# Statistics and score placement in the memory-attention stage of a decoder layer: q statistics ahead of the mix statistics, scores ahead of the up product, denominators behind it

## The chip, the cores and the metric

The program runs on all 8 cores of one Trainium2 chip. Each core computes one of the eight batch elements, all cores run the same instructions on data of their own, and the weights are shared. The metric is device time in microseconds (us) of the slowest core, the median of several executions; lower is better.

## The reference

One decoder layer over 4096 positions of width 1024: a mixer of gated linear attention and dilated window attention, then cross-attention into 256 memory tokens, then a gated MLP. The change lies in the second of the three, and in its overlap with the end of the first and the start of the third:

```python
def memory_cross_attention(h, mem, ...):
    xn = rms_norm(h, norm_x)
    mn = rms_norm(mem, norm_mem)
    q = rms_norm((xn @ w_xq).reshape(b, s, X_HEADS, X_HEAD_DIM), x_q_norm)
    k, v = jnp.split(mn @ w_xkv, 2, axis=-1)
    k = rms_norm(k.reshape(b, m, X_HEADS, X_HEAD_DIM), x_k_norm)
    p = jax.nn.softmax(jnp.einsum('bshd,bmhd->bhsm', q, k) * (X_HEAD_DIM ** -0.5), axis=-1)
    o = jnp.einsum('bhsm,bmhd->bshd', p, v).reshape(b, s, D_MODEL)
    return h + o @ w_xo
```

Before it stands `h + merged @ w_mix_out` (the mix), behind it `up = rms_norm(h) @ w_ffn_up`, a causal convolution of width 3 on the gate half, `gelu(conv) * u`, and the down product.

## The kernel before

The 4096 positions are cut into 32 tiles of 128 (`NT = 32`) and 8 blocks of 512. Every engine has one instruction list in program order; an instruction waits on semaphores for the writers of what it reads and for the readers of what it overwrites, and everything behind it on that engine waits too. So the order of the Python calls is the order on each engine, and nothing is scheduled later. All matmuls are recorded by one helper line (L249), ScalarE activations by L275, VectorE tensor-tensor operations by L282, scalar-tensor-tensor by L308, plain DMAs by L241, DMA transposes by L245.

The memory stage is a software pipeline, the loop `for k in range(5, NT + 11)` (L1817). In step k it works on several tiles and heads at once:

- `mix(i)` (L1412), only for k < 9, tiles 28 to 31: 16 matmuls of 512 columns, two VectorE adds into the tile `xt` (xtT in the trace), its store as h1, then the mix statistics: a ScalarE Square over 1024 columns with an accumulated sum (junkT), `rstd_pool` (two short GpSimd operations), and the VectorE scaling to `xs` (xsT). `x2trans` and `x2store` transpose xs by DMA through one buffer x2s and store it, `x2load` (L1534) reads it back (x2i) for the q product two steps on.
- `q_proj(k)` (L1562): 16 matmuls into two of the three PSUM banks of `PQ`. `q_stats(k)` (L1574): four Squares of 256 columns, Ln, Exp on ScalarE (jh, hnx). `q_norm(k)`: four VectorE operations that read the two banks (qn). `q_trans(k)`: a DMA transpose to qT.
- `score` (L1688) for head index k-5, a block and one of its four heads: 4 matmuls and two ScalarE Exps into a `ptsx` buffer (three of them). `denom` (L1700): 2 matmuls of a matrix of ones with ptsx, then Ln and Exp on ScalarE (lgx, rdx). `outp` (L1711): VectorE multiplies ptsx by the reciprocal denominator (pn).
- `x_out(k-10)` (L1718), the output product: 16 matmuls, two VectorE adds into the tile h1x, a store.
- From k = 32 on there is no q product. In its place stands `up(0, fc)` (L1774), 16 matmuls of the first MLP block: one ScalarE copy of the gate half (abt), which shares a buffer with a short VectorE copy of the history columns (hist) and so comes behind it, then VectorE's convolution (cv). `glu` (L1797) of the column group before does the Gelu on ScalarE (gl) and a VectorE product (yT), which frees the bank of the other half.

I call k = 32 to 36 the tail: in these five steps scores 27 to 31 are made beside `up` 0 to 4. Before the change a tail step issues on TensorE: `denom` of the last step's score, `x_out`, `up`, `score`. The banks of `score`, `denom` and `x_out` come from one rotation `P` of five; those of `up` from `PQ`. At k = 37 `P` becomes a rotation of all eight and `up` joins it; counted through, `up(5)` then gets the bank that the second half of `x_out(27)` has just filled, and `x_out(28)` gets the bank of the other half of `up(4)`. In steps 37 to 41 the four last output products run with `up` 5 to 13; after that the rest of the MLP.

Of the kernel before, what the change touches and what calls it, by code (L numbers as in the profile page):

```python
# [407 lines left out]
NT = S // 128  # L408
# [31 lines left out]
def build():  # L440
# [47 lines left out]
    def rows(i):  # L488
        return slice(i * 128, (i + 1) * 128)
# [42 lines left out]
    def rstd_pool(ss, src, dst, n, dim):  # L532
        fw.ts("pool", ss[:, dst:dst + n], ss[:, src:src + n], 1.0 / dim, ALU.mult, EPS, ALU.add)
        fw.tt("pool", ss[:, dst:dst + n], ss[:, dst:dst + n], mh[:, 0:n], ALU.pow)
# [632 lines left out]
    for c in range(NT):  # L1167
        s_, c4 = c // 4, c % 4
        nx = 1 <= s_ < NS - 1
        i = c + 8  # L1170
# [56 lines left out]
    TA = [dict() for _ in range(NT)]  # L1227
# [180 lines left out]
    def xload(i):  # L1408
        TA[i]["xt"] = xtr.next()
        fw.dma(TA[i]["xt"][:, :], x[rows(i), :])  # L1410

    def mix(i):  # L1412
        s_, t_ = i // 4, i % 4
        h1t = TA[i]["xt"]
        for half in range(2):
            cs_ = slice(half * 512, (half + 1) * 512)
            pm = P.next()
            for kc in range(8):
                fw.mm(pm[:, :], mT[s_ % 2][:, kc, t_ * 128:(t_ + 1) * 128], wmo[:, kc, cs_], start=(kc == 0), stop=(kc == 7))
            fw.tt("dve", h1t[:, cs_], pm[:, :], h1t[:, cs_], ALU.add)  # L1420
        fw.dma(V(h1_d[i], h1_d[i].t[rows(i), :]), h1t[:, :])
        ss = ogc["nss"].next()
        fw.act(ogc["junk"][:, :], h1t[:, :], AF.Square, accum=ss[:, 0:1])
        rstd_pool(ss, 0, 2, 1, 1024)
        xs = ogc["xs"].next()
        fw.ts("dve", xs[:, :], h1t[:, :], ss[:, 2:3], ALU.mult)
        TA[i]["xs"] = xs

    def x2trans(i):
        fw.dmat(x2s[:, :, :], TA[i]["xs"][:, :])  # L1430

    def x2store(i):
        fw.dma(V(xn2_d[i], xn2_d[i].t[i]), x2s[:, :, :].rearrange("p c t -> p (c t)"))
# [100 lines left out]
    def x2load(i):  # L1534
        TC[i]["x2"] = ogc["x2i"].next()
        fw.dma(TC[i]["x2"][:, :, :].rearrange("p c t -> p (c t)"), V(xn2_d[i], xn2_d[i].t[i]))
# [25 lines left out]
    def q_proj(i):  # L1562
        c = TC[i]
        xnv = c["x2"]
        pq = []
        for half in range(2):
            cs_ = slice(half * 512, (half + 1) * 512)
            p_ = PQ.next()
            for kc in range(8):
                fw.mm(p_[:, :], xnv[:, kc, :], KV["wxq"][kc // 2][:, kc % 2, cs_], start=(kc == 0), stop=(kc == 7))  # L1570
            pq.append(p_)
        c["qs"] = [pq[h // 2][:, (h % 2) * 256:(h % 2 + 1) * 256] for h in range(4)]

    def q_stats(i):  # L1574
        ss = QA["hnr"].next()
        for h in range(4):
            fw.act(V(QA["jhs"][h], QA["jh"].t[:, h, :]), TC[i]["qs"][h], AF.Square, accum=ss[:, h:h + 1])
        fw.act(ss[:, 4:8], ss[:, 0:4], AF.Ln, scale=1.0 / 256, bias=eps_c)
        TC[i]["ss"] = ss
        return fw.act(ss[:, 8:12], ss[:, 4:8], AF.Exp, scale=-0.5)  # L1580

    def q_norm(i):
        c = TC[i]
        qn = QA["qn2r"].next()
        for h in range(4):
            fw.stt("dve", qn[:, h * 256:(h + 1) * 256], c["qs"][h], c["ss"][:, 8 + h:9 + h], KV["gq"][:, :],
                   ALU.mult, ALU.mult)
        c["qn"] = qn

    def q_trans(i):  # L1590
        fw.dmat(QA["qTs"][i // 4 % 2][i % 4][:, :, :], TC[i]["qn"][:, :])
# [24 lines left out]
    for s_ in range(NS):  # L1616
        for m in range(8):
# [18 lines left out]
            if L % 2 == 1 and 8 <= (L + 9) // 2 < NT:  # L1636
                i = (L + 9) // 2
# [3 lines left out]
            if s_ > 0:  # L1641
                i = (s_ - 1) * 4 + m // 2
# [37 lines left out]
    def t1b_late():  # L1680
        XL["pn"].append([ar.at("pn1_%d" % h, (128, 2, 512), BF16, (120 + 2 * h) * K_) for h in range(4)])
        XL["xsr"] = ar_ring("xsX", 2, (128, 1024), BF16, 128 * K_)
        XL["junkX"] = ar.at("junkX", (128, 1024), BF16, 134 * K_)
# [4 lines left out]
    def score(s_, h):  # L1688
        pts = ptsr.next()
        for mb in range(2):  # L1690
            p_ = PB.next()
            for dc in range(2):
                ap = QA["qT"][s_ % 2].t[:, :, h * 2 + dc, :]
                v_ = [V(b, ap) for b in QA["qTs"][s_ % 2]]
                fw.mm(p_[:, :], kmT[:, h * 2 + dc, mb * 128:(mb + 1) * 128], v_[0], start=(dc == 0), stop=(dc == 1),
                      xr=v_[1:])
            fw.act(pts[:, mb, :], p_[:, :], AF.Exp, scale=1.0 / 16)
        SC[s_][h] = pts

    def denom(s_, h):  # L1700
        pts = SC[s_][h]
        pD = PB.next()
        for mb in range(2):
            fw.mm(pD[:, :], ones_b, pts[:, mb, :], start=(mb == 0), stop=(mb == 1))
        lg = XL["lgr"].next()
        fw.act(lg[:, :], pD[:, :], AF.Ln)
        rd = XL["rdr"].next()
        fw.act(rd[:, :], lg[:, :], AF.Exp, scale=-1.0)
        SC[s_]["rd"] = rd

    def outp(s_, h):  # L1711
        fw.tt("dve", XL["pn"][s_ % 2][h][:, :, :], SC[s_][h][:, :, :], SC[s_]["rd"][:, :].raw(0, [[0, 2], [1, 512]]), ALU.mult)
# [5 lines left out]
    def x_out(i):  # L1718
        s_, t_ = i // 4, i % 4
        c = TC[i]  # L1720
        h_ = c["h"]
        pn = XL["pn"][s_ % 2]
        for half in range(2):
            cs_ = slice(half * 512, (half + 1) * 512)
            px = PB.next()
            for kc in range(8):
                fw.mm(px[:, :], pn[kc // 2][:, kc % 2, t_ * 128:(t_ + 1) * 128], KV["MX"][kc // 2][:, kc % 2, cs_],
                      start=(kc == 0), stop=(kc == 7))
            fw.tt("dve", h_[:, cs_], px[:, :], h_[:, cs_], ALU.add)
        fw.dma(V(h2_d[i], h2_d[i].t[rows(i), :]), h_[:, :])  # L1730

    def x_stats(i):
        c = TC[i]
        h_ = c["h"]
        jk, ss = XL["junkX"], XL["nsr"].next()
        fw.act(jk[:, :], h_[:, :], AF.Square, accum=ss[:, 0:1])
        fw.act(ss[:, 1:2], ss[:, 0:1], AF.Ln, scale=1.0 / 1024, bias=eps_c)
        fw.act(ss[:, 2:3], ss[:, 1:2], AF.Exp, scale=-0.5)
        c["xss"] = ss
# [7 lines left out]
    def x3_trans(i):  # L1747
        fw.dmat(F_["x3s"][i % 4][:, :, :], TC[i]["xs"][:, :])
# [48 lines left out]
    def glu(p):  # L1797
        fc, c1, pu = p
        gl = F_["gl"].next()
        fw.act(gl[:, :], c1[:, :], AF.Gelu)  # L1800
        fw.tt("dve", ysub[fc][:, :], gl[:, :], pu[:, :], ALU.mult)
# [15 lines left out]
    for k in range(5, NT + 11):  # L1817
        pace = None
        if k < 9:
            if k < 8:  # L1820
                xload(NT - 3 + k - 5)
            mix(NT - 4 + k - 5)
        if k < 10:
            x2trans(NT - 5 + k - 5)
        if k == 9:
            t1b_late()
        if k < NT:
            q_proj(k)
            pace = q_stats(k)
        if 0 <= k - 6 < NT:  # L1830
            denom((k - 6) // 4, (k - 6) % 4)
        if 0 <= k - 5 < NT and k < NT:
            score((k - 5) // 4, (k - 5) % 4)
        if 6 < k + 2 < NT:
            x2load(k + 2)
        if k < NT:
            q_norm(k)
            q_trans(k)
        if k < 10:
            x2store(NT - 5 + k - 5)  # L1840
        if 0 <= k - 6 < NT:
            outp((k - 6) // 4, (k - 6) % 4)
        if 0 <= k - 10 < NT:
            x_out(k - 10)
        if k >= NT:
            if k == NT:
                ffn_alloc()
            if k == NT + 5:
                P.items = BK[3:8] + BK[0:3]
                PF["r"] = P  # L1850
            for _ in range(1 if k < NT + 6 else 2):
                if len(UPD) < 14:
                    cur = up(0, len(UPD))
                    if UPD:
                        glu(UPD[-1])
                    UPD.append(cur)
            if k - 5 < NT:
                score((k - 5) // 4, (k - 5) % 4)
        if 0 <= k - 10 < 4:
            x_stats(k - 10)  # L1860
            x_scale(k - 10)
            x3_trans(k - 10)
        if pace is not None:
            fw.wait_for("pool", [pace])
        if 0 <= k - 8 < NT:
            loadh(k - 8)
        if 9 <= k < NT + 1 and k % 2 == 1:
            up_load((k - 9) // 4, (k - 9) // 2 % 2)
        for fc in UP_LATE.get(k - NT, ()):
            up_load(fc)  # L1870
        if k == NT + 5:
            wdn_load(0)
        if k == NT + 6:
            wdn_load(1)
        if k == NT + 7:
            wdn_load(2)
# [26 lines left out]
    for s_ in range(NS):  # L1903
# [12 lines left out]
        for t_ in range(4):  # L1916
            i = s_ * 4 + t_
# [69 lines left out]
```

How the kernel before makes its waits and increments, by code:

```python
            def run(eng, acts, s):  # L368
                for a in acts:
                    if a[0] == "w":
                        eng.wait_ge(a[1], a[2])
                    else:
                        ins = a[1]
                        bi = ins.fn(eng)
                        if ins.dma:
                            bi.then_inc(dsem[ins.dsem], 16)
                        elif ins.signal:
                            bi.then_inc(esem[s], 1)
```

## Time and profile before

| what | value |
|---|---|
| median of 3 runs | 2854.3 us (2852.8 to 3007.62) |
| the profiled execution's own time | 2852.89 us |
| its span, core 0, the slowest | 2851.3 us (the cores: 2839.6 to 2851.3) |
| TensorE busy | 2752.4 us (97%), 15208 matmuls |
| VectorE, ScalarE, GpSimd busy | 1734.0 us (61%), 1220.7 us (43%), 1032.3 us (36%) |
| TensorE's share of the chain that ended last | 86% |
| mean granted TensorE clock of core 0 | 0.992 |

The span runs from the first to the last instruction of a core; the 1.6 us between the profiled execution's time and its span lie around it. Times within the trace are counted from the start of the span. PE is TensorE, DVE VectorE, ACT ScalarE, POOL GpSimd. In a table by stretch each engine has its busy time with the number of instructions in brackets, then come the granted clock as a share of 2.4 GHz, the busy share of the DMA engines and GB/s; a timeline row has the start, the duration, engine, line, operation, and what is written from what. A row's number in square brackets is idle time of the engine before the instruction, with what ended it. A TensorE row's duration holds a modelled pipeline end, so rows overlap by some 0.17 us.

### The profile page before, as it was taken

Reading aid. Unit: us, or ns where it says so; the run is one execution under the profiler, and the core shown is the slowest. Engines: PE = TensorE matmul, PEld = TensorE weight load, DVE = VectorE, ACT = ScalarE, POOL = GpSimd, SP = SyncE. Lnnn points to the kernel's source line nnn. Section 1 sums busy time; section 2 is a strip of 40 time slices with the busy share of each in tenths; the row PEclk is TensorE's granted clock in tenths of the full one; section 3 lists DMA queues with packets and bytes.
Section 4 is the critical chain, followed back from the end, with each engine's and each line's share of the span. In section 5 each row is a group of like instructions: output and inputs, shape, how many; then the busy total and the mean of one; then the engine's idle time right before and its main releaser. Section 6 shows DMA issues by size and latency. Waiting matters only on the chain.

```text
span 2851.3 us, 51345 instructions; the slowest of 8 cores (2839.6 to 2851.3 us)
## 1 busy us (share of the span) xinstructions
PE 2752.4 (97%) x15208; PEld 1328.2 (47%) x15208; DVE 1734.0 (61%) x2716; ACT 1220.7 (43%) x2438; POOL 1032.3 (36%) x1592
## 2 busy tenths in 40 slices
PE   7899999999999999999999989989999999999998
PEld 3444445665555444444444434434444444444443
DVE  4777775777887885344433355556566575575663
ACT  5666654555666665222323466552222232232221
POOL 1577667777777775222224300011111111111110
PEclk8999999999999999999999999999999999999999
DMA  8377644667788776466977488867412303213110
GB/s 163 98 136 139 126 86 92 119 122 132 155 154 163 153 162 181 113 146 163 166 159 158 130 221 219 213 217 171 135 31 74 104 2 103 60 45 104 32 58 37
DMA packets 394341, 359.47 MB, mean 126 GB/s; under 512 B 308328, under 2 KB 312180, under 8 KB 393204
## 3 DMA queue, kind: packets, MB, share of 16 engines
q1 hardware_dynamic: 367616, 261.17, 37.6%
q0 software_dynamic: 25584, 94.57, 16.8%
q8 instruction: 127, 2.08, 0.3%
q10 hardware_dynamic: 868, 0.47, 0.2%
q14 instruction: 146, 1.20, 0.1%
HBM read 241.20 MB, written 111.94 MB: 124 GB/s over the span
## 4 chain that ended last, share of the span: by engine, by line
PE 86%; DMA 3%; DVE 3%; issue 3%; ACT 2%; POOL 1%; SPq 1%; DVEq 0%; ACTq 0%; POOLq 0%
PE psum L249 86%; SPq L245 1%; DMA wkv_224<-w_xkv 1%; DMA xtT_216<-x 0%; DVE cm_72 L312 0%; ACT L275 0%; DMA x2s<-xsT_218 0%; ACT junkA L275 0%; DMA qkT_164<-qkb_160 0%; DMA oat<-oa_d 0%; DVE G_141 L282 0%; DVE G_142 L282 0%; DMA kTa<-ke_3_84 0%; DMA xt_61<-x 0%; DMA kTb<-ke_3_92 0%
## 5 line engine op out<-in xcount | busy, mean ns | idle before, releaser
L317 ACT COPY abt_289<-psum 128x512 f32<-128x512 f32 x88 | 51.7, 587 | 317.8 <-PE psum L249 317.8
L317 ACT COPY abt_290<-psum 128x512 f32<-128x512 f32 x88 | 51.7, 588 | 219.2 <-PE psum L249 208.6
L318 POOL COPY hist<-abt_289 128x2 f32<-128x2 f32 x81 | 14.9, 184 | 327.2 <-ACT abt_289 L317 327.2
L282 DVE TENSOR_TENSOR qg_150<-psum,gqk 128x512 f32<-128x512 f32 x96 | 65.7, 685 | 65.8 <-ACT sq_147 L275 39.4
L282 DVE TENSOR_TENSOR qg_149<-psum,gqk 128x512 f32<-128x512 f32 x96 | 65.7, 685 | 63.8 <-ACT sq_147 L275 54.4
L249 PE MATMUL psum<-wd_0_144,xnT 128*128 128x512 bf16 x384 | 103.7, 393 | 0.0
L318 POOL COPY hist<-abt_290 128x2 f32<-128x2 f32 x81 | 15.0, 185 | 238.6 <-ACT abt_290 L317 238.6
L282 DVE TENSOR_TENSOR mab_206<-psum,sig_205 128x512 f32<-128x512 f32 x56 | 38.6, 689 | 101.9 <-PE psum L249 101.8
L249 PE MATMUL psum<-wd_0_182,xnT 128*128 128x512 bf16 x384 | 100.4, 384 | 0.0
L249 PE MATMUL psum<-wd_1_145,xnT 128*128 128x512 bf16 x384 | 99.4, 382 | 0.0
L249 PE MATMUL psum<-wd_0_184,xnT 128*128 128x512 bf16 x384 | 99.2, 381 | 0.0
L249 PE MATMUL psum<-wd_1_185,xnT 128*128 128x512 bf16 x384 | 98.5, 379 | 0.0
L249 PE MATMUL psum<-wd_1_183,xnT 128*128 128x512 bf16 x384 | 98.5, 379 | 0.0
L282 POOL TENSOR_TENSOR mT_214<-mab_206,mab_207 128x512 bf16<-128x512 f32 x32 | 40.4, 1264 | 147.0 <-DVE mab_206 L282 80.1
L275 ACT ACTIVATE sq_148<-psum 128x512 f32<-128x512 f32 x96 | 57.6, 600 | 82.0 <-PE psum L249 82.0
L300 DVE TENSOR_SCALAR cv_0_284<-abt_289,gall 128x512 f32<-128x512 f32 x88 | 48.0, 546 | 67.5 <-ACT abt_289 L317 67.5
L282 POOL TENSOR_TENSOR mT_202<-mab_206,mab_207 128x512 bf16<-128x512 f32 x32 | 40.8, 1274 | 127.8 <-DVE mab_206 L282 67.9
L300 DVE TENSOR_SCALAR cv_1_285<-abt_290,gall 128x512 f32<-128x512 f32 x88 | 48.1, 546 | 61.8 <-ACT abt_290 L317 61.8
L275 ACT ACTIVATE sig_205<-psum,gall 128x512 f32<-128x512 f32 x61 | 42.0, 689 | 100.9 <-PE psum L249 100.9
L275 ACT ACTIVATE sq_147<-psum 128x512 f32<-128x512 f32 x96 | 57.4, 598 | 60.7 <-PE psum L249 60.7
L282 DVE TENSOR_TENSOR mab_207<-psum,sig_204 128x512 f32<-128x512 f32 x56 | 38.4, 686 | 65.4 <-ACT sig_204 L275 54.3
L275 ACT ACTIVATE sig_204<-psum,gall 128x512 f32<-128x512 f32 x61 | 41.7, 683 | 83.6 <-PE psum L249 81.5
(889 smaller groups left out, 7739.4 us busy)
## 6 DMA issues: line engine op xcount, KB each, us to landing
wub_d<-w_up POOLq DMA_DIRECT2D x22, 512.0 KB, 6.0
og_d<-og_176 SPq DMA_DIRECT2D x32, 260.0 KB, 2.6
og_d<-og_177 SPq DMA_DIRECT2D x32, 260.0 KB, 3.1
og_d<-og_178 SPq DMA_DIRECT2D x32, 260.0 KB, 2.5
oga_180<-og_d SPq DMA_DIRECT2D x32, 260.0 KB, 3.2
oa_d<-on_112 POOLq DMA_DIRECT2D x32, 256.0 KB, 2.5
xtT_215<-x SPq DMA_DIRECT2D x16, 512.0 KB, 4.6
h_d<-xtT_215 SPq DMA_DIRECT2D x16, 512.0 KB, 2.9
```

The lines of the kernel that those rows point to most:

```text
L245: return self._add("sp", lambda e: e.dma_start_transpose(out=o, in_=i), [in_], [out], dma=True, xr=xr)
L249: return self._add("pe", lambda e: e.matmul(o, l, r, start=start, stop=stop), [lhsT, rhs], [out], xr=xr)
L275: return self._add("act", lambda e: e.activation(o, i, func, **kw), reads, writes, xr=xr, xw=xw)
L282: return self._add(eng, lambda e: e.tensor_tensor(o, a, b, op), [in0, in1], [out], xr=xr, xw=xw)
L300: return self._add(eng, lambda e: e.tensor_scalar(o, a, s1, s2, op0, **kw), reads, writes)
L317: return self._add("act", lambda e: e.copy(o, i), [in_], [out])
L318: return self._add(eng, lambda e: e.tensor_copy(o, i), [in_], [out])
```

## The change

Two edits in the loop of the memory stage, and `mix` is split so that its statistics can be called apart (`mix_stat`).

First, for k = 5 to 8, `mix` no longer issues its statistics; `mix_stat` is called behind `q_stats`, ahead of `denom` and `score`.

Second, for k >= 32, `score` goes from behind `up` to between `x_out` and `up`; `denom` and `outp` of that score go from the next step to the end of the same step, behind `up`.

```diff
+    def mix_stat(i):
+        h1t = TA[i]["xt"]
         ss = ogc["nss"].next()
         fw.act(ogc["junk"][:, :], h1t[:, :], AF.Square, accum=ss[:, 0:1])
...
-            mix(NT - 4 + k - 5)
+            mix(NT - 4 + k - 5, False)
...
             q_proj(k)
             pace = q_stats(k)
-        if 0 <= k - 6 < NT:
+        if k < 9:
+            mix_stat(NT - 4 + k - 5)
+        if 0 <= k - 6 <= NT - 6:
             denom((k - 6) // 4, (k - 6) % 4)
...
-        if 0 <= k - 6 < NT:
+        if 0 <= k - 6 <= NT - 6:
             outp((k - 6) // 4, (k - 6) % 4)
         if 0 <= k - 10 < NT:
             x_out(k - 10)
         if k >= NT:
+            if k - 5 < NT:
+                score((k - 5) // 4, (k - 5) % 4)
...
             if k - 5 < NT:
-                score((k - 5) // 4, (k - 5) % 4)
+                denom((k - 5) // 4, (k - 5) % 4)
+                outp((k - 5) // 4, (k - 5) % 4)
```

The lists of VectorE, GpSimd and the DMA queues keep their order; only TensorE's and ScalarE's differ. On TensorE in the tail, here at k = 34 (the rows with wxo and pn are the end of `x_out`, qTx and kmT the score, wup the up product, ptsx the denominator):

```order
 L249 MATMUL psum<-wxo_229,pn_2_264 128x512 x2
 L249 MATMUL psum<-wxo_230,pn_3_265 128x512 x2
+L249 MATMUL psum<-qTx_249,kmT 128x512 x4
 L249 MATMUL psum<-x3T,wup_280 128x512 x16
-L249 MATMUL psum<-qTx_249,kmT 128x512 x4
 L249 MATMUL psum<-ptsx_252,cstb 128x512 x2
 L249 MATMUL psum<-mx_232,pn_0_262 128x512 x2
```

The four score matmuls stand 16 matmuls earlier; the two of the denominator keep their place between the up product and the next output product, although another step now calls them.

On ScalarE in the tail, here at k = 33 (lgx and rdx are the denominator's Ln and Exp, abt the copy of the gate half, gl the Gelu, ptsx the scores' Exps):

```order
 L275 ACTIVATE rdx_261<-lgx_259 128x512
-L317 COPY abt_290<-psum 128x512
-L275 ACTIVATE gl_287<-cv_0_284 128x512
 L275 ACTIVATE ptsx_251<-psum 128x512 x2
+L317 COPY abt_290<-psum 128x512
+L275 ACTIVATE gl_287<-cv_0_284 128x512
 L275 ACTIVATE lgx_258<-psum 128x512
 L275 ACTIVATE rdx_260<-lgx_258 128x512
```

The copy and the Gelu go from ahead of the scores' Exps to between these and the denominator.

On ScalarE at the start of the loop, here at k = 6 (junkT is the mix statistic, jh and hnx the q statistics):

```order
-L275 ACTIVATE junkT,nssT_195<-xtT_216 128x1024
 L275 ACTIVATE jh,hnx_243<-psum 128x256 x4
 L275 ACTIVATE hnx_243<-hnx_243,epsb 128x4
 L275 ACTIVATE hnx_243<-hnx_243 128x4
+L275 ACTIVATE junkT,nssT_195<-xtT_216 128x1024
 L275 ACTIVATE lgx_258<-psum 128x512
 L275 ACTIVATE rdx_260<-lgx_258 128x512
 L275 ACTIVATE ptsx_251<-psum 128x512 x2
```

The mix statistic goes behind the six instructions of the q statistics. On VectorE the scaling to xs still stands ahead of `q_norm`.

## Rows read from the trace of the kernel before

**Rows 1.** Table by stretch, core 0: busy per engine, TensorE's granted clock, DMA share, GB/s

```profile
1865.00:1938.00 73.00, 57.38 (x246) 24.33 (x245) 35.00 (x59) 31.79 (x43) 12.70 (x25) 0.95 0.74 229
```

**Rows 2.** Waits of TensorE, 1700 to 2300 us, core 0: total, times, longest

```profile
PE psum L249 <- ACT ptsx_251 L275: 5.7, 2, 2.8
PE psum L249 <- ACT ptsx_250 L275: 3.9, 2, 2.8
PE psum L249 <- ACT ptsx_252 L275: 2.8, 1, 2.8
PE psum L249 <- DVE yT_296 L282: 2.2, 1, 2.2
```

**Rows 3.** Table by stretch again: tail steps k = 32, 34 and 35 of core 0

```profile
1865.46:1874.92 9.46, 8.36 (x39) 3.66 (x38) 6.78 (x11) 3.01 (x5) 0.36 (x1) 1.00 0.91 277
...
1886.12:1897.31 11.19, 8.36 (x38) 3.65 (x39) 5.31 (x9) 6.21 (x8) 2.11 (x4) 1.00 0.61 177
1897.31:1910.19 12.88, 10.05 (x39) 4.06 (x39) 5.40 (x9) 6.21 (x8) 2.11 (x4) 0.87 0.79 282
```

**Rows 4.** TensorE's timeline in the tail and behind it, core 0

```profile
1890.00 3.62 PE L249 MATMUL psum<-x3T,wup_280 128*128 128x512 bf16 x16
1893.45 1.03 PE L249 MATMUL psum<-qTx_249,kmT 128*128 128x512 bf16 x4
1897.31 0.59 PE L249 MATMUL psum<-ptsx_252,cstb 128*128 128x512 bf16 x2 [2.83 <-ACT ptsx_252 L275]
...
1921.38 0.59 PE L249 MATMUL psum<-ptsx_251,cstb 128*128 128x512 bf16 x2 [2.83 <-ACT ptsx_251 L275]
...
1928.13 3.61 PE L249 MATMUL psum<-x3T,wup_283 128*128 128x512 bf16 x16 [1.01 <-DVE abt_290 L318]
```

**Rows 5.** ScalarE's timeline in the tail, k = 34 and 35, core 0

```profile
1892.04 0.59 ACT L317 COPY abt_289<-psum 128x512 f32<-128x512 f32 x1 [3.91 <-PE psum L249]
1892.64 1.28 ACT L275 ACT_TABLE_LOAD   x1
1893.93 0.63 ACT L275 ACTIVATE gl_288<-cv_1_285 128x512 f32<-128x512 f32 x1
1894.58 1.28 ACT L275 ACT_TABLE_LOAD   x1
...
1898.00 0.60 ACT L275 ACTIVATE lgx_259<-psum 128x512 f32<-128x512 f32 x1 [0.83 <-PE psum L249]
```

**Rows 6.** VectorE's timeline in the tail, core 0

```profile
1899.42 1.23 DVE L282 TENSOR_TENSOR pn_1_272<-ptsx_252,rdx_261 128x1024 bf16<-128x1024 bf16 x1 [3.77 <-ACT rdx_261 L275]
...
1927.29 0.69 DVE L282 TENSOR_TENSOR h1x_257<-psum,h1x_257 128x512 f32<-128x512 f32 x1 [1.50 <-PE psum L249]
1927.90 0.23 DVE L318 COPY abt_290<-hist 128x2 f32<-128x2 f32 x1
```

**Rows 7.** TensorE's timeline at the start of the loop, core 0

```profile
1669.29 0.59 PE L249 MATMUL psum<-wxq_235,x2i_239 128*128 128x512 bf16 x2 [1.04 <-DVE qn_1_247 L308]
...
1678.65 0.59 PE L249 MATMUL psum<-wxq_235,x2i_237 128*128 128x512 bf16 x2 [1.92 <-DVE qn_2_248 L308]
...
1691.80 0.59 PE L249 MATMUL psum<-wxq_235,x2i_239 128*128 128x512 bf16 x2 [1.35 <-DMA x2i_239<-xn_d]
```

**Rows 8.** TensorE's timeline at the same place on core 3

```profile
1676.78 1.01 PE L249 MATMUL psum<-wxq_235,x2i_237 128*128 128x512 bf16 x2 [4.43 <-DVE qn_2_248 L308]
```

**Rows 9.** ScalarE's timeline at k = 8, core 0: mix statistic, first of the q statistics

```profile
1673.35 1.06 ACT L275 ACTIVATE junkT<-xtT_216 128x1024 bf16<-128x1024 f32 x1 [3.07 <-DVE xtT_216 L282]
...
1674.41 0.36 ACT L275 ACTIVATE jh<-psum 128x256 bf16<-128x256 f32 x1
```

**Rows 10.** VectorE's timeline at k = 8, core 0

```profile
1675.73 0.75 DVE L300 TENSOR_SCALAR xsT_218<-xtT_216,nssT_193 128x1024 bf16<-128x1024 f32 x1 [2.52 <-POOL nssT_193 L282]
1677.43 2.25 DVE L308 SCALAR_TENSOR_TENSOR qn_2_248<-psum,hnx_245,gqx 128x256 bf16<-128x256 f32 x4 [0.95 <-ACT hnx_245 L275]
```

**Rows 11.** DMAs of the buffer x2s, 1640 to 1695 us, core 0

```profile
DMA to landing us min/median/max: 2.1/4.2/9.9
```

More of the change, by code:

```diff
@@ L1410, in xload, with mix @@
         fw.dma(TA[i]["xt"][:, :], x[rows(i), :])
-    def mix(i):
+    def mix(i, stat=True):
         s_, t_ = i // 4, i % 4
@@ L1421, in mix @@
         fw.dma(V(h1_d[i], h1_d[i].t[rows(i), :]), h1t[:, :])
+        if stat:
+            mix_stat(i)
+    def mix_stat(i):
+        h1t = TA[i]["xt"]
         ss = ogc["nss"].next()
```

## The prediction

> **What bounds the kernel now.** Read the table by engine first: TensorE is busy for 97% of the span and carries 86% of the chain that ended last. A change pays here only if it removes idle time of TensorE or lets its clock stay up. So the next view is TensorE's own waits in the stretch that the second edit touches [rows 2]. They are few: five waits for the Exps of a score (ptsx), 12.4 us together, and one of 2.2 us at k = 38 that the change leaves alone. The table by stretch shows the price step by step: a tail step takes 11.19 us, one takes 12.88 [rows 3]. In the one of 12.88 the granted clock has a mean of 0.87, in its neighbour 1.00; part of that step ran at 1.2 instead of 2.4 GHz. The timeline shows the cause of the waits: the score's matmuls are followed at once by the denominator, which needs both Exps [rows 4]. On ScalarE these Exps stand behind the copy, a table load of 1.28 us, the Gelu and a second load [rows 5].
>
> At the start of the loop TensorE waits for the banks that `q_norm` reads, and for x2i by DMA [rows 7]; other cores wait longer at the same place, core 3 once for 4.43 us [rows 8].
>
> **Second edit, the tail.** One matmul of 512 columns takes 3.45/16 = 0.216 us (from 1890.00 to 1893.45, [rows 4]). A tail step has 2 + 16 + 16 + 4 = 38 of them: 8.20 us if nothing waits. With the score ahead of `up`, 16 matmuls (3.45 us) lie between the score and its denominator. ScalarE's two Exps, about 0.6 us each like the Ln [rows 5], then start without copy, loads and Gelu ahead of them, and end within this cover. If the cover were gone, the wait of 2.83 would stand as it is.
>
> Removed: k = 32 falls from 9.46 to 8.20, that is 1.26. Of the other four, k = 34 is the pattern (11.19 - 8.20 = 2.99), k = 35 has the same wait and 12.88 - 11.19 = 1.69 of slow clock on top. So 1.26 + 4 x 2.99 + 1.69 = 14.9 us.
>
> What is late next? `denom`'s Ln now stands behind copy, load, Gelu, load. Counted from the start of `up`: copy at 2.04 (1890.00 to 1892.04), second load over at 5.86 (1895.86), hence the Ln; pn 1.42 behind the Ln's start (1898.00 to 1899.42) at 7.28, over at 8.51; the two VectorE adds of the next `x_out`, 0.69 each, queued behind pn, at 8.51 and 9.20; then the history copy, 0.61 behind the second add's start and 0.23 long at most, over at 10.04 [rows 4 to 6]. The next `up`'s copy is due at 8.20 + 2.04 = 10.24. This ring has 0.2 us of slack, so I take the steps at 8.20 and charge nothing; if the slack is short by as much again it costs 0.2 x 4 = 0.8.
>
> At k = 37 there is no slack, since `up(5)` takes the bank of the second half of `x_out(27)`. TensorE went on 0.84 after the start of that add (1927.29 to 1928.13, [rows 4, 6]). The add now starts 9.20 after `up(4)`, so `up(5)` starts at 10.04, where its 34 matmuls between (16 + 2 + 16) would allow 7.34: a wait of 2.7. From the denominator's start to `up(5)` it was 1928.13 - 1921.38 = 6.75, which holds the wait of 1.01 and a second slow-clock stretch (this piece has 18 matmuls, 3.89, and 1.01 + 0.17 of wait with the modelled end, so 1.7 is the clock). Now it is 3.89 + 2.7 = 6.6. Gain 0.15. The tail sums to 14.9 + 0.15 = 15.1 us. Behind it nothing changes: the later loads are issued in GpSimd's unchanged order and wait for events that come earlier by the same amount, and each up weight is used several steps after its load. The DMA share of the stretch is 0.74 [rows 1]; squeezed from 73 to 58 us the same traffic is 0.93, still under one.
>
> The slow clock could also come back: 2.7 of wait at k = 37 and the unchanged 2.2 at k = 38 lie 3.5 us apart, and two of the four waits of 2.83 were followed by one. That is 1.7 us, left in the range.
>
> **First edit, k = 5 to 8.** At k = 8 ScalarE sat 3.07 us until the mix's adds were done, did the Square (1.06), and only then the q statistics, though q_proj's banks were full by 1669.29 + 8 x 0.216 = 1671.0 [rows 7, 9]. Put first, the q statistics use that idle time. But VectorE keeps xs ahead of `q_norm`, and xs (1675.73, 0.75 long) does not move, as the adds still release the Square. `q_norm` can start at 1676.48 instead of 1677.43: a gain of 0.95 [rows 10], which halves TensorE's bank wait of 1.92. Where the adds are early instead, the Square comes up to 3.0 us later (the six q instructions, 1674.41 to `q_norm`'s start at 1677.43), xs with it, and `q_norm` behind xs: before, it started 4.1 after the Square could start (1673.35 to 1677.43), now 3.0 + 2.4 + 0.75 = 6.15 (2.4 from the Square's start to xs), so 2.1 later. Bounds for four steps: a loss of 8, against a gain of the two bank waits, 3.0 on core 0, and 4.43 plus 1.7 of clock on core 3 [rows 7, 8].
>
> Yet the stretch ends on another wait: at 1691.80 `q_proj(11)` waits 1.35 us for x2i, the end of the xs, transpose, store, load chain through the single x2s buffer [rows 7]. What TensorE gains before that point it waits there, unless the chain itself is shorter, and the chain runs on landings of 2.1 to 9.9 us [rows 11]. I take a gain of 0.5 us, near the nothing that this row suggests for the slowest core.
>
> **Sum.** 2852.89 - 15.1 - 0.5 = 2837.3 us against the profiled execution, which stands 1.4 below the median of the runs shown.
>
> **Rivals.** *ScalarE's ring sets the tail step.* For it: the ring's 0.2 us of slack. Against it: ScalarE is busy only 6.21 of 11.19 us [rows 3]. If the new order needs one more table load per step, 1.28, the step is 8.20 + 1.1 = 9.3 and four steps give back 4.4: 2841.7. If each of the two switches cost 1.28 more, the step is 8.20 + 2.4 = 10.6, 9.4 back: 2846.7. In the row of before the Gelu starts 0.01 us after the load's end, so a switch costs 1.28 and no more [rows 5].
> The Trainium skill, "ScalarE: Activation LUTs", section "What ACT_TABLE_LOAD costs", says otherwise: a load of about 1283 ns and a drain of about 1380 ns with it, 2.66 us for each switch. The load agrees with the row, the drain is not seen there; by the page the step would be an estimated 8.20 + 2.76 - 0.2 = 10.8 us and the time about 2847.5.
>
> *The first edit gains more.* For it: core 3's 4.43 us and the clock after it. If the chain over x2s follows the earlier `q_norm`, the slowest core keeps its 3.0 us of bank waits: 2834.8. Against it: the wait at 1691.80.
>
> *The removed waits come back at the loads.* For it: DMA share 0.93. If the squeezed tail's loads land later than TensorE asks, all 12.4 us of score waits return as DMA waits: 2849.7. Against it: several steps between load and use.
>
> *The first edit costs more than the tail gives.* `q_trans` is issued sooner and so stands right beside the transposes of x2s, on which the next load waits. If the four x2s transposes behind it land at the longest 9.9 us instead of the median 4.2 [rows 11], the chain is 4 x 5.7 = 22.8 us longer, and TensorE waits it out before `q_proj(11)`: 2837.8 + 22.8 = 2860.6, slower than before. It decides from 15.1 us on. Against it: the order of the DMA queue does not change, and the bytes do not either.
>
> *The change does nothing to the waits*, because the Exps still come too late. Three times 0.6 against 3.45 us of cover speaks against it; I count it with the loads.
>
> **Chances.** Forecast 0.77; first edit gains more 0.09; ring 0.07; loads 0.04; slower 0.03. The likeliest case alone spans 2832 to 2843 (a slow-clock stretch more or less, the first edit's smaller bounds, some 3 us between executions). Reaching to the case of the larger gain below and to the rings and loads above I give 2828 to 2848. A measurement of this kernel can tell about 2% from no change, some 57 us, and every case but mishaps outside these lies within: within 2% 0.97, faster 0.01, slower 0.02.
>
> **What would show it.** Right: no TensorE wait on ptsx in the tail, steps of 8.2 us, granted clock 1.00 through k = 36, and a wait of about 2.7 us ahead of `up(5)`. ScalarE's row shows two table loads a step, the Ln directly behind the second. At the start of the loop `q_norm` waits for xs, not for hnx, and `q_proj(11)` still waits for x2i. Wrong: tail steps of 9 us or more with VectorE's pn late; waits on wup or h1x; a wait for x2i that grew by more than the bank waits fell.

## The result, and the profile after

The changed kernel takes 2839.9 us (median of 4 runs, lowest 2836.5) against 2857.9 us (median of 4, lowest 2852.8) for the kernel before: a ratio of 0.9939, 95% interval [0.9911, 0.9967], that is 17 us of some 2855, and under the 2% that count as a change. The forecast was 2837.3 us in a range of 2828 to 2848.

The slowest core changes from run to run, and on the chips of the experiments many executions had one die at a mean clock of about 0.98 and some 20 us longer. So beside each ratio I give the **die median**: the median span of a die's four cores, averaged over all dies whose four clocks were at least 0.987, with its standard error. The kernel before has 2847.4 ± 0.3 (38 dies), 2847.9 ± 0.3 (33) and 2848.2 ± 0.4 (15) on the three chips of the experiments. In the profiled execution beside the changed kernel its two dies had 2847.9 and 2848.3, the changed kernel's seven 2831.6 ± 0.6 in the mean: 16.5 us less, and 15.8 to 16.6 less than the kernel before on the other three chips.

The traces tell where. From `up(6)` to the end every core takes 914.0 us in both kernels, and ahead of `q_proj(4)` the two programs are the same (the cores of the kernel before start it at 1621.6 to 1633.9 us, those of the changed one at 1626.0 to 1632.6). Between these two points a core takes 304.5 us in the mean before and 288.8 after: 15.6 us less, 14.6 of them from `x_out(22)`, where the tail begins, to `up(6)` (71.9 before, 57.2 after).

**The tail.** The table by stretch, core 0, four successive steps from denominator to denominator (columns as in [rows 1, 3]), and behind them a longer stretch, the counterpart of the 73 us of [rows 1]:

```profile
1864.41:1872.61 8.20, 8.20 (x40) 3.72 (x38) 4.72 (x9) 3.82 (x6) 2.61 (x6) 1.00 0.91 306
1872.61:1880.81 8.20, 8.20 (x39) 3.72 (x38) 5.44 (x10) 6.20 (x9) 2.11 (x4) 1.00 0.54 169
1880.81:1889.01 8.20, 8.20 (x39) 3.72 (x38) 5.36 (x10) 6.20 (x9) 1.38 (x3) 1.00 0.93 334
1889.01:1897.21 8.20, 8.20 (x39) 3.72 (x38) 5.37 (x10) 6.20 (x9) 2.84 (x6) 1.00 0.94 279
1864.41:1922.00 57.59, 53.15 (x238) 23.50 (x237) 33.60 (x59) 30.78 (x41) 12.64 (x25) 0.97 0.89 266
```

Where [rows 3] had 9.46, 11.19 and 12.88 us, each step now takes 8.20, TensorE is busy in all of it, and the granted clock is 1.00. The last row's 0.97 shows that the clock falls behind these steps. TensorE's timeline, core 0, says where:

```profile
1876.49 1.03 PE L249 MATMUL psum<-qTx_249,kmT 128*128 128x512 bf16 x4
1877.36 3.62 PE L249 MATMUL psum<-x3T,wup_280 128*128 128x512 bf16 x16
1880.81 0.59 PE L249 MATMUL psum<-ptsx_252,cstb 128*128 128x512 bf16 x2
...
1893.76 3.62 PE L249 MATMUL psum<-x3T,wup_282 128*128 128x512 bf16 x16
...
1903.82 5.30 PE L249 MATMUL psum<-x3T,wup_283 128*128 128x512 bf16 x16 [2.56 <-DVE abt_290 L318]
1911.00 0.59 PE L249 MATMUL psum<-mx_232,pn_0_271 128*128 128x512 bf16 x2 [1.88 <-DVE yT_296 L282]
```

The denominator at 1880.81 no longer waits for its ptsx; the row with 2.83 in [rows 4] is its counterpart. Ahead of `up(5)` the wait has grown from 1.01 to 2.56 us, and the 16 matmuls behind it take 5.30 instead of 3.61: the granted clock from 1903.82 to 1909.00 is 0.67, so part of them ran at 1.2 GHz. On the 8 cores this row takes 3.6 us on three and up to 5.3 on five. From the start of `x_out(22)` to that of `up(5)` it is 47.2 us on every core, where before it was 60.5 to 63.9; from there to `up(6)` it is 9.25 to 10.8, before 9.25 or 10.93.

ScalarE's timeline for the same steps, core 0:

```profile
1877.19 1.29 ACT L275 ACTIVATE ptsx_252<-psum 128x512 bf16<-128x512 f32 x2 [0.83 <-PE psum L249]
1879.39 0.59 ACT L317 COPY abt_289<-psum 128x512 f32<-128x512 f32 x1 [0.92 <-PE psum L249]
1880.00 1.28 ACT L275 ACT_TABLE_LOAD   x1
1881.29 0.63 ACT L275 ACTIVATE gl_288<-cv_1_285 128x512 f32<-128x512 f32 x1
1881.94 1.28 ACT L275 ACT_TABLE_LOAD   x1
1883.23 0.60 ACT L275 ACTIVATE lgx_259<-psum 128x512 f32<-128x512 f32 x1
1883.92 0.63 ACT L275 ACTIVATE rdx_261<-lgx_259 128x512 f32<-128x512 f32 x1
```

and VectorE's, core 0:

```profile
1884.66 1.23 DVE L282 TENSOR_TENSOR pn_1_272<-ptsx_252,rdx_261 128x1024 bf16<-128x1024 bf16 x1 [1.59 <-ACT rdx_261 L275]
1885.80 1.48 DVE L282 TENSOR_TENSOR h1x_255<-psum,h1x_255 128x512 f32<-128x512 f32 x2
1887.19 0.16 DVE L318 COPY abt_290<-hist 128x2 f32<-128x2 f32 x1
...
1902.20 1.48 DVE L282 TENSOR_TENSOR h1x_257<-psum,h1x_257 128x512 f32<-128x512 f32 x2
1903.59 0.16 DVE L318 COPY abt_290<-hist 128x2 f32<-128x2 f32 x1
```

The two Exps now stand ahead of the copy ([rows 5] had them behind both loads), two loads a step remain, and the Ln follows the second at once. The history copy is over at 1887.35, and the next step's ScalarE copy, 8.20 behind the 1879.39 shown, starts at 1887.60: the ring has some 0.2 us to spare.

**The start of the loop.** TensorE's waits there, core 0, up to k = 15:

```profile
1664.94 0.75 PE L249 MATMUL psum<-wxq_235,x2i_237 128*128 128x512 bf16 x2 [2.62 <-DMA x2i_237<-xn_d]
...
1672.89 0.59 PE L249 MATMUL psum<-wxq_235,x2i_238 128*128 128x512 bf16 x2 [1.36 <-DVE qn_0_246 L308]
...
1708.89 0.59 PE L249 MATMUL psum<-wxq_235,x2i_239 128*128 128x512 bf16 x2 [1.12 <-DVE qn_1_247 L308]
...
1718.51 0.59 PE L249 MATMUL psum<-wxq_235,x2i_237 128*128 128x512 bf16 x2 [1.26 <-DVE qn_2_248 L308]
```

and VectorE at k = 8, core 0, the counterpart of [rows 10]:

```profile
1665.43 0.75 DVE L300 TENSOR_SCALAR xsT_218<-xtT_216,nssT_193 128x1024 bf16<-128x1024 f32 x1 [2.52 <-POOL nssT_193 L282]
1666.10 2.24 DVE L308 SCALAR_TENSOR_TENSOR qn_2_248<-psum,hnx_245,gqx 128x256 bf16<-128x256 f32 x4
```

`q_norm` now starts directly behind xs. Summed up to k = 11 and averaged over the eight cores, TensorE's waits for qn fall from 5.1 to 1.3 us and those for x2i rise from 1.6 to 4.0. From `q_proj(4)` to `q_proj(12)` it is 66.1 us in the mean before and 64.5 after. The two waits for qn at 1708 and 1718 (k = 14 and 15) stand on seven of the eight cores, with one on the eighth; behind k = 11 such waits are 2.3 us in the mean, where before they were 1.8. Before, x2i was waited for at k = 9 on four cores and at k = 11 on six (core 0: [rows 7]); now at k = 9 on all eight, at k = 10 on five, and at k = 11 on core 3 alone. The slowest core shows the worst case of x2i, TensorE's timeline, core 7:

```profile
1680.89 1.01 PE L249 MATMUL psum<-wxq_235,x2i_238 128*128 128x512 bf16 x2 [3.97 <-DMA x2i_238<-xn_d]
1681.69 1.06 PE L249 MATMUL psum<-wxq_233,x2i_238 128*128 128x512 bf16 x2
```

Two matmuls take 0.85 us from start to start there instead of 0.43: the granted clock from 1681 to 1685 us is 0.50, so the lower clock followed the wait of 3.97 us.

### The profile page after: what moved, and what is told of

It reads as the page before. It is cut to its first block, busy times and chain, and to the rows that moved or that the text cites. A ratio compares the mean times of both kernels' runs of the same rounds, so it can differ in the third digit from the quotient of the medians.

```text
span 2838.9 us, 51340 instructions; the slowest of 8 cores (2826.0 to 2838.9 us)
## 1 busy us (share of the span) xinstructions
PE 2756.7 (97%) x15208; PEld 1331.0 (47%) x15208; DVE 1733.1 (61%) x2716; ACT 1218.9 (43%) x2438; POOL 1036.7 (37%) x1592
## 4 chain that ended last, share of the span: by engine, by line
PE 90%; DMA 3%; DVE 2%; issue 2%; ACT 1%; POOL 1%; SPq 1%; DVEq 0%; ACTq 0%; POOLq 0%
PE psum L249 90%; SPq L245 1%; DMA x2s<-xsT_218 0%; DMA xtT_216<-x 0%; DMA kTa<-ke_3_84 0%; DMA xn_d<-x2s 0%; DMA oat<-oa_d 0%; DMA grow<-gvec 0%; DMA x2i_238<-xn_d 0%; DVE G_141 L282 0%; PE psum L253 0%; DVE G_142 L282 0%; DMA kTb<-ke_3_92 0%; POOL on_112 L282 0%; ACT junkA L275 0%
## 5 line engine op out<-in xcount | busy, mean ns | idle before, releaser
L275 ACT ACTIVATE sig_205<-psum,gall 128x512 f32<-128x512 f32 x61 | 41.9, 687 | 101.0 <-PE psum L249 101.0
L275 ACT ACTIVATE jh<-psum 128x256 bf16<-128x256 f32 x128 | 49.0, 383 | 79.4 <-PE psum L249 73.0
L282 DVE TENSOR_TENSOR mab_207<-psum,sig_204 128x512 f32<-128x512 f32 x56 | 38.5, 687 | 68.9 <-ACT sig_204 L275 57.8
```

The lines of the kernel that those rows point to most:

```text
L275: return self._add("act", lambda e: e.activation(o, i, func, **kw), reads, writes, xr=xr, xw=xw)
L282: return self._add(eng, lambda e: e.tensor_tensor(o, a, b, op), [in0, in1], [out], xr=xr, xw=xw)
```

## The experiments

| kernel | die median, dies | against before | ratio of medians, 95% |
|---|---|---|---|
| changed kernel | 2831.6 ± 0.6 (7) | -16.5 | 0.9939 [0.9911, 0.9967] |
| 1: first edit alone | 2845.5 ± 0.6 (13) | -1.9 ± 0.7 | 0.9965 [0.9927, 1.0003] |
| 2: second edit alone | 2833.2 ± 0.3 (12) | -14.2 ± 0.4 | 0.9948 [0.9914, 0.9982] |
| 3: other bank order at k = 37 | 2825.1 ± 0.4 (8) | -22.3 ± 0.5 | 0.9950 [0.9905, 0.9994] |
| 4: denominator directly behind the score | 2842.0 ± 0.4 (16) | -5.4 ± 0.5 | 0.9951 [0.9919, 0.9983] |
| 5: x_stats one step later | 2829.2 ± 0.4 (20) | -18.6 ± 0.5 | 0.9936 [0.9903, 0.9970] |
| 6: 3 and 5 together | 2822.2 ± 0.7 (10) | -25.7 ± 0.7 | 0.9896 [0.9848, 0.9944] |
| 7: xs behind q_norm | 2831.9 ± 0.3 (18) | -16.0 ± 0.4 | 0.9954 [0.9922, 0.9985] |
| 8: an Exp twice (one execution) | - | - | - |
| 9: as 4, table load early | 2835.0 ± 0.6 (14) | -13.2 ± 0.7 | 0.9940 [0.9900, 0.9980] |

Each difference is to the kernel before on the same chip; that of the changed kernel rests on only two dies of the kernel before, so its error is larger than the others'.

### 1 and 2: each edit alone

Experiment 1 is the kernel before with the first edit (and `mix` split for it):

```diff
-            mix(NT - 4 + k - 5)
+            mix(NT - 4 + k - 5, False)
...
             pace = q_stats(k)
+        if k < 9:
+            mix_stat(NT - 4 + k - 5)
```

Experiment 2 is the changed kernel with these lines taken back, so that only the tail is changed.

> The first edit alone (mix statistics behind the q statistics at k = 5 to 8), the tail as before. My theory: nearly all of the gain of 15 to 18 us lies in the tail, so this kernel is 0 to 2 us faster than before (ratio 0.9993 to 1.0000); TensorE's waits for qn at k = 8 and 9 fall by 2 to 4 us a core, waits for x2i grow by about as much, and the five waits for ptsx stay at 12.4 us. Rival: the first edit is worth 3 us or more by itself (ratio 0.999 or lower), since most cores lost a 4.4 us wait for qn. Second rival: it costs 2 us or more, since core 7 of the changed kernel waited 4.0 us for x2i.

> The second edit alone (scores behind the output product, denominators behind the up product for k >= 32), the start of the loop as before. My theory: 13 to 15 us faster than before (ratio 0.9947 to 0.9955), no wait for ptsx, tail steps of 8.20 us, a wait of 2.6 us ahead of up(5), and from up(0) to up(6) 52.1 us on cores without a slow-clock stretch, 53.5 with one; the waits for qn at k = 8 and 9 as before. Rival: the first edit gave 3 us or more, so this one is only 11 us or less faster.

Measured: -1.9 and -14.2 us, together -16.1, and the changed kernel has -16.5. Within the noise the edits add up. In 1 the five ptsx waits stand as in [rows 2] (12.4 to 12.8 us), and the qn waits up to k = 11 are 0 to 2.6 a core. From `q_proj(4)` to `q_proj(12)` it takes 64.9 us in the mean over the cores, and experiment 2, without the first edit, takes 66.5: both much as in the result (64.5 with the edit, 66.1 without). The trace of 1 is nevertheless no shorter up to `up(6)` than before (305.0 and 304.5 us from `q_proj(4)`), since its tail met more of the slow clock (73.3 us from `x_out(22)`, before 71.9); so the size of this small gain rests on the die medians. In 2 the tail is as in the changed kernel (47.2 us to `up(5)` on all cores), but every core then takes 9.8 to 10.9 us to `up(6)`; the qn waits are as before, up to 6.1. From `x_out(22)` to `up(6)` it is 57.7 us in the mean where before it was 71.9: the 14.2 of the die medians.

### 3: other banks at k = 37

The changed kernel, with the rotation of eight banks begun in such an order that `up(5)` and `x_out(28)` get banks that have long been read:

```diff
             if k == NT + 5:
-                P.items = BK[3:8] + BK[0:3]
+                P.items = [BK[q] for q in (3, 4, 5, 2, 6, 7, 0, 1)]
+                P.i = 0
```

> The changed kernel with another order of the eight PSUM banks from k = 37 on, so that up(5) and x_out(28) get banks that were freed long before. My theory: the wait of 2.6 us ahead of up(5) is VectorE's add of x_out(27), queued behind pn, and the one of 1.8 to 2.2 us ahead of x_out(28) is the glu product; both go, and with them the slow-clock stretch in up(5), so 4.5 to 6.3 us less than the changed kernel (about 20 us less than before). Rival: the waits move on to the next bank or to ScalarE's copy, and less than 1.5 us are gained.

Measured: 22.3 us under the kernel before where the changed kernel is 16.5 under it: 5.8 more. (The 7.0 us that the expectation of experiment 6 names leaves out one of the changed kernel's seven dies, and compares across chips; with that die it is 6.5.) TensorE's timeline from `up(5)` on, core 2 of this kernel:

```profile
1896.24 1.24 PE L249 MATMUL psum<-wxo,pn 128*128 128x512 bf16 x5
1897.32 3.62 PE L249 MATMUL psum<-x3T,wup 128*128 128x512 bf16 x16
1900.78 0.59 PE L249 MATMUL psum<-mx,pn 128*128 128x512 bf16 x2
```

No wait is left at `up(5)` (1897.32) nor at `x_out(28)` (1900.78), and no slow clock on any core: from `x_out(22)` to `up(6)` it is 44.46 + 6.91 = 51.4 us on all eight, against 56.4 to 58.0 in the changed kernel, 5.8 less in the mean. On cores without a slow stretch the difference is 5.1 us, the two waits (2.56 + 2.2, with a little beside them); on the others the clock comes on top. So the wait ahead of `up(5)` belongs to the bank that `x_out(27)`'s add reads, and not to the history copy that the trace names as its releaser; that one is merely the last event ahead of it.

### 4 and 9: the denominator directly behind the score

```diff
             if k - 5 < NT:
                 score((k - 5) // 4, (k - 5) % 4)
+                denom((k - 5) // 4, (k - 5) % 4)
...
             if k - 5 < NT:
-                denom((k - 5) // 4, (k - 5) % 4)
                 outp((k - 5) // 4, (k - 5) % 4)
```

> The changed kernel with the denominator's matmuls and its Ln and Exp ahead of the up product, right behind the score; outp stays behind up. This has the scores' Exps ahead of copy and Gelu on ScalarE, but no up product as cover. My theory: each of the five tail steps waits 1.1 us for ptsx, as k = 33 of the kernel before did, where no Gelu was due: 8.20 + 1.26 = 9.5 us a step, +6 us, against a wait ahead of up(5) that falls from 2.6 to at most 1, so 3 to 5 us slower than the changed kernel. If the cover is what counts the wait is 2.8 us as before, +13 us; if only the order on ScalarE counts it is near 0.

Measured: 5.4 us under the kernel before, so 11.1 less than the changed kernel gains, more than twice the price expected (3 to 5). The trace agrees: from `x_out(22)` to `up(6)` it is 68.2 us in the mean over the cores, and 57.2 in the changed kernel. The ptsx waits sum to 9.3 to 9.5 us a core; the theory had 1.1 us for each of the five, and three of them are 2.38. TensorE's timeline, core 6 of this kernel, the denominators at k = 33 and 34:

```profile
1872.99 0.59 PE L249 MATMUL psum<-ptsx,cstb 128*128 128x512 bf16 x2 [1.10 <-ACT ptsx L275]
...
1883.73 0.59 PE L249 MATMUL psum<-ptsx,cstb 128*128 128x512 bf16 x2 [2.38 <-ACT ptsx L275]
```

and ScalarE's, same core:

```profile
1877.36 0.63 ACT L275 ACTIVATE gl<-cv 128x512 f32<-128x512 f32 x1
1881.01 1.28 ACT L275 ACT_TABLE_LOAD   x1 [3.02 <-PE psum L249]
1882.30 1.29 ACT L275 ACTIVATE ptsx<-psum 128x512 bf16<-128x512 f32 x2
```

ScalarE is idle for 3.02 us behind the Gelu, and yet the Exps' table load starts only when the score's bank is full. It has no input of its own, but it stands behind the wait of the activation that needs it. 1.10 + 1.28 = 2.38 is the longer wait. If that is the cause, an Exp that needs nothing, put behind the Gelu, must draw the load into the idle time. That is experiment 9:

```diff
                     if UPD:
                         glu(UPD[-1])
+                        if k < NT + 4:
+                            fw.act(XL["nsr"].next()[:, 0:1], eps_c, AF.Exp)
                     UPD.append(cur)
```

> The order with the denominator directly behind the score (the fourth experiment), plus an Exp of one column behind each of the Gelus at k = 33 to 35; it writes a spare tile and needs nothing but a constant. Its row in the trace there showed the Exps' table load standing behind the wait for the score, so that its 1.28 us come after the score's matmuls. Theory (the load waits with the activation that needs it): the load moves into ScalarE's idle time behind the Gelu, three ptsx waits fall from 2.38 to about 1.10, the tail is 3.8 us shorter and the span too, to some 2838 us in the median core of an undisturbed die. Rival (the 2.38 us come from the two Exps and the modelled ends, wherever the load stands): the waits stay at 2.38 and the span at 2842.

TensorE's timeline, core 6 of this kernel:

```profile
1871.80 0.59 PE L249 MATMUL psum<-ptsx,cstb 128*128 128x512 bf16 x2 [1.10 <-ACT ptsx L275]
...
1881.25 0.59 PE L249 MATMUL psum<-ptsx,cstb 128*128 128x512 bf16 x2 [1.10 <-ACT ptsx L275]
```

and ScalarE's:

```profile
1876.16 0.63 ACT L275 ACTIVATE gl<-cv 128x512 f32<-128x512 f32 x1
1876.81 1.28 ACT L275 ACT_TABLE_LOAD   x1
1878.10 0.20 ACT L275 ACTIVATE nsX<-epsb 128x1 f32<-128x1 f32 x1
1879.82 1.29 ACT L275 ACTIVATE ptsx<-psum 128x512 bf16<-128x512 f32 x2 [1.52 <-PE psum L249]
```

All five waits are 1.10 us now (5.5 to 5.7 a core). From `x_out(22)` to `up(5)` it is 52.2 us, against 57.8 on core 0 of experiment 4: 3.84 of the 5.6 are the three loads, the rest a slow-clock stretch of 1.7 that came with the waits of 2.38 and does not come with those of 1.10. The waits went as the theory said; the gain against before grows from 5.4 to 13.2 us where 3.8 more was expected. From `x_out(22)` to `up(6)` the trace shows 5.9 us in the mean over the cores (68.2 and 62.3), loads and clock. The traces show no more that the edit could give: from `q_proj(4)` to `up(6)` they differ by 5.5 us (298.6 and 293.1), behind it both take 914.0, and ahead of it the programs are the same. Why the die medians differ by 7.8 stays open.

### 5 and 6: the statistics of x_stats one step later

The two qn waits at k = 14 and 15 come where the first four output tiles get their own statistics (junkX), which stand ahead of the next step's q statistics on ScalarE. Experiment 5 applies to them what the first edit does to the mix's statistics; 6 adds the bank order of 3.

```diff
+        if 0 <= k - 11 < 4:
+            x_stats(k - 11)
         if 0 <= k - 10 < NT:
             x_out(k - 10)
+        if 0 <= k - 11 < 4:
+            x_scale(k - 11)
+            x3_trans(k - 11)
...
-        if 0 <= k - 10 < 4:
-            x_stats(k - 10)
-            x_scale(k - 10)
-            x3_trans(k - 10)
```

> The changed kernel, with the statistics of x_stats at k = 10 to 13 taken one step later: on ScalarE behind the next step's score, with their scaling on VectorE behind the next step's h1x adds. So the q statistics of k = 11 to 14 stand ahead of the Square of x_stats, as the first edit does with the mix's statistics. Theory A (a ring of ScalarE and VectorE, h1x add, Square, q statistics, q_norm, pn, next h1x add, sets steps of 9.64 us at k = 11 to 14 and gives back part of what the first edit gained): TensorE's waits for qn behind k = 12, 1.1 us at k = 13 and again at k = 14 on nearly every core of the changed kernel, go, and the span falls by 2 to 2.5 us. Rival B (TensorE's work has slack there, or the wait returns at the next transpose or at xs of the FFN): the qn waits go or halve, but another takes their place, and the span moves by less than 1 us.

> The same edit together with the other bank order at k = 37, which took 7.0 us off the changed kernel. If the two are independent: 9 to 9.5 us under the changed kernel, some 25 under the kernel before. If the time gained at k = 13 and 14 is lost again in the stretch up to the tail: 7 us under the changed kernel, as the bank order alone.

ScalarE's timeline in the changed kernel, core 0, the Square of x_stats at k = 11 to 13:

```profile
1693.29 1.06 ACT L275 ACTIVATE junkX<-h1x_255 128x1024 bf16<-128x1024 f32 x1 [2.39 <-DVE h1x_255 L282]
...
1702.92 1.06 ACT L275 ACTIVATE junkX<-h1x_256 128x1024 bf16<-128x1024 f32 x1 [2.66 <-DVE h1x_256 L282]
...
1712.54 1.06 ACT L275 ACTIVATE junkX<-h1x_257 128x1024 bf16<-128x1024 f32 x1 [2.66 <-DVE h1x_257 L282]
```

and in experiment 5, core 3, the first Square of the q statistics of three steps:

```profile
1693.21 0.39 ACT L275 ACTIVATE jh<-psum 128x256 bf16<-128x256 f32 x1 [0.54 <-PE psum L249]
...
1701.42 0.38 ACT L275 ACTIVATE jh<-psum 128x256 bf16<-128x256 f32 x1 [0.59 <-PE psum L249]
...
1709.62 0.38 ACT L275 ACTIVATE jh<-psum 128x256 bf16<-128x256 f32 x1 [0.59 <-PE psum L249]
```

In the changed kernel ScalarE waits for VectorE's adds and the period is 9.63 us; in experiment 5 it waits for TensorE, and the period is 8.2. TensorE's waits from k = 12 to the tail fall from 2.3 us in the mean over the cores to nothing, and from `q_proj(12)` to `q_proj(31)` it is 155.8 us on every core where the changed kernel has 158.4 in the mean: 2.6 gained there. The slow clock at `up(5)`, in this trace on seven cores and not five, took back 0.6 (57.8 us from `x_out(22)` to `up(6)`, not 57.2). The die median is 18.6 us under before where the changed kernel is 16.5: 2.1 gained, as the 2 to 2.5 expected. With the bank order it is 25.7 against 22.3 of experiment 3, 9.2 more than the changed kernel, as expected of two independent edits (9 to 9.5). This version, at 2832.4 us (median of 6, lowest 2826.1) and a ratio of 0.9896, is under both kernels.

### 7: xs behind q_norm

At k = 5 to 8 VectorE is idle for 2.5 us ahead of xs (the row at 1665.43 above), and `q_norm` takes 2.24.

```diff
             q_norm(k)
+            if k < 9:
+                mix_scale(NT - 4 + k - 5, mss)
             q_trans(k)
```

(`mix_scale` is the last part of `mix_stat`, which no longer does it.)

> The changed kernel with xs, the mix's scaling on VectorE, behind q_norm at k = 5 to 8. In the changed kernel q_norm starts right behind xs, and VectorE is idle for 2.5 us ahead of xs, so the four products of q_norm (2.24 us) fit into that idle time and xs hardly moves. Theory A (the bank wait is real, but the x2s chain ends last): the rest of the qn waits at k = 6 to 9 (0.2 to 2.6 us a core) goes, the waits for x2i grow by as much, and the span stays within 0.7 us. Rival B (the bank waits themselves set the end): the span falls by 1 to 2 us and x2i waits stay at 2.2 to 6.1 us.

Measured: -16.0 us, within the noise the changed kernel's own gain (16.5). On four cores the qn waits up to k = 11 are gone and those for x2i are 5.0 to 6.2; on the other four 1.5 to 3.2 of qn are left, with 2.3 to 5.9 of x2i. All waits of TensorE up to there sum to 5.8 us in the mean over the cores, 5.7 in the changed kernel. What is taken from the bank wait is paid at x2i. Why four cores keep a qn wait was not pursued.

### 8: how much slack the ring has

The Exp of the reciprocal denominator is done twice in the tail; the values stay the same.

```diff
         fw.act(rd[:, :], lg[:, :], AF.Exp, scale=-1.0)
+        if twice:
+            fw.act(rd[:, :], lg[:, :], AF.Exp, scale=-1.0)
```

> The changed kernel with the Exp that makes 1/sum (rdx) done twice in each denominator of the tail, k = 32 to 36; the second writes the same values. It lengthens ScalarE's part of the ring by 0.54 to 0.63 us. Theory of the prediction (the ring of copy, two loads, Gelu, Ln, Exp, pn, h1x adds and history copy has 0.2 us of slack against the 8.20 of TensorE): the steps grow to about 8.5 to 8.6 us, TensorE waits 0.3 to 0.4 us a step, and the wait ahead of up(5) grows from 2.56 to about 3.1. Rival (ScalarE's copy of up does not wait for VectorE's history copy, so the ring has more slack): the steps stay at 8.20 and only the wait ahead of up(5) grows.

ScalarE's copies in the tail, core 0 of this kernel:

```profile
1871.90 0.59 ACT L317 COPY abt<-psum 128x512 f32<-128x512 f32 x1 [0.92 <-PE psum L249]
...
1880.67 0.59 ACT L317 COPY abt<-psum 128x512 f32<-128x512 f32 x1 [1.49 <-DVE abt L318]
...
1889.44 0.59 ACT L317 COPY abt<-psum 128x512 f32<-128x512 f32 x1 [1.72 <-DVE abt L318]
...
1898.21 0.59 ACT L317 COPY abt<-psum 128x512 f32<-128x512 f32 x1 [1.72 <-DVE abt L318]
```

and TensorE's two rows at `up(4)` and `up(5)`:

```profile
1894.47 3.62 PE L249 MATMUL psum<-x3T,wup 128*128 128x512 bf16 x16
...
1906.96 5.53 PE L249 MATMUL psum<-x3T,wup 128*128 128x512 bf16 x16 [4.99 <-DVE abt L318]
```

The copy waits for VectorE's history copy, as the prediction had it, and the ring turns in 8.77 us. The extra Exp adds 0.72 (two take 1.35, one 0.63), so without it the ring needs 8.05, 0.15 under the 8.20 of TensorE. Yet TensorE does not wait in any step: its steps stay at 8.20, ScalarE falls behind by 0.57 a step, and the whole debt, 3 x 0.57 + 0.72 = 2.43 us, falls due at `up(5)`, where the wait is 4.99 instead of 2.56 (4.98 to 5.09 on the eight cores). The theory was right on the ring and wrong on where its price shows.

## Why the prediction was right, step by step

**The tail's steps: right.** Four steps of 8.20, no wait for ptsx, clock 1.00 through k = 36. From `x_out(22)` to `up(5)` core 0 takes 47.2 us instead of 62.2: 15.0, where the terms sum to 14.9 + 0.15.

**The ring of ScalarE and VectorE: right.** Counted from the start of `up(2)` at 1877.36, the prediction put the Ln at 5.86, pn at 7.28, the end of the history copy at 10.04. Measured: 5.87 (1883.23), 7.30 (1884.66), 9.99 (1887.35). Its slack of 0.2 is 0.15 by experiment 8. So the first rival (the ring sets the step) did not come about, but by a margin of 0.15 us: an operation of 0.72 us more costs 2.43. Its dearer variant fell with the row at 1881.29, a Gelu that starts 0.01 us behind the load's end. The Trainium skill, "ScalarE: Activation LUTs", section "What ACT_TABLE_LOAD costs", adds a drain of some 1380 ns to a load of 1283; the trace agrees on the load (1.28) and shows no drain.

**The wait ahead of `up(5)`: right in size, its clock went the other way.** Forecast 2.7, measured 2.56. The term of 0.15 at k = 37 supposed that the second slow-clock stretch goes; the prediction named its return (1.7 us) and left it in the range. It came back behind the wait, in part or whole, on five of eight cores in the changed kernel and on all eight in experiment 2 (9.8 to 10.9 us to `up(6)` instead of 9.25). That takes the gain of the second edit from 15.1 to 14.6 in the changed kernel's trace, and to 14.2 ± 0.4 in experiment 2.

**The first edit: sign right, size probably too small.** Forecast 0.5, measured 1.9 ± 0.7 alone by die medians; the trace of the changed kernel shows 15.6 - 14.6 = 1.0. `q_norm` stands directly behind xs, as worked out, and x2i takes back a part: qn down by 3.8 us, x2i up by 2.4 in the mean. The step that failed is the one on `q_proj(11)`, "What TensorE gains before that point it waits there": on seven of eight cores no such wait is left there; it comes at k = 9 and 10, and is not the full toll. That x2i is nevertheless the limit at this place experiment 7 shows: where a qn wait goes by another means, x2i wait takes its place, and the span does not move. The prediction also looked no further than `q_proj(11)`. The ring through x_stats costs 2.6 us up to k = 15 (experiment 5); most of that stood there before, and some 0.5 us of the first edit's gain went into it (from `q_proj(12)` to `q_proj(31)` 157.9 us before, 158.4 after).

**The sum.** 15.6 us forecast, 15.6 by the traces between `q_proj(4)` and `up(6)`, 16.5 by die medians. That it fits so closely is luck: the tail gave 0.5 to 0.9 us less than its term, the first edit 0.5 to 1.4 more, and the two errors cancel. The profiled execution, 2840.5 us, is only 12.4 under the one of before, since its slowest core, 7, met the 3.97 us x2i wait and the slow clock behind it; cores 0 to 6 end at 2826 to 2837.

**The other rivals.** The waits did not come back at the loads: no wait of TensorE in the tail names a DMA, although the DMA share rose to 0.94 in single steps (0.93 was the forecast for the mean, 0.89 it is). Nor did the x2s chain grow by 22.8 us: x2i waits rose by 2.4 in the mean, and sum to 6.1 on the worst core.

## What to carry to other kernels

When a wait is removed from a software pipeline, follow the ring that carries the debt (here ScalarE's loads, pn, adds, history copy) to the first place where the fast engine needs one of its buffers at once: the price shows there in one lump, and not in the steps. There, look at who gets which bank: with the order of eight bank numbers alone 5.8 us were to be had, two fifths of what the whole second edit gave. And an edit that pays at one place of a loop (q statistics ahead of another statistic) is worth looking for at every other place where the same two stand in the same order.

## What the runs showed of the hardware that I had not expected

A table load on ScalarE stands behind the wait of the activation that needs it, although it has no input: 3.02 us of idle time passed ahead of the load of 1.28 in experiment 4, and a one-column Exp of 0.20 us in front took it out of the way in experiment 9. Whether the engine holds the load back or the program has it behind the wait, these runs do not tell. In the changed kernel the same load adds no wait to TensorE: it starts 0.02 us behind the Gelu, and the Ln 0.01 us behind it.

A wait can cost more than its length, where a stretch at the lower clock follows it. Five waits of some 1.10 us in successive steps were followed by none (experiment 9: 52.2 or 52.3 us to `up(5)` on all cores, granted clock 1.00 there on core 6); with three of 2.38 among them there were one or two of 1.7 us each on every core (experiment 4: 57.7 to 59.4 us, granted clock 0.97 on core 6). Behind the pair at k = 37 and 38 (2.56 and about 2.2) one came on five cores of eight in the changed kernel, on all eight in experiment 2 and on seven in experiment 5; behind the shorter pair of experiment 9 (1.26 and 2.2) on four; with both waits gone, on none (experiment 3). Why the same waits draw it on one core and not on another the runs do not show.
